# Down projections by seven half-size products whose weight and token sums GpSimd makes

## The reference

```python
x = x + 0.5 * swiglu(rmsnorm(x, g_ffn1), w1_gate, w1_up, w1_down)
x = x + concat(sparse_attention, latent_attention) @ w_out
x = x + 0.5 * swiglu(rmsnorm(x, g_ffn2), w2_gate, w2_up, w2_down)
return rmsnorm(x, g_final)

def swiglu(x, w_gate, w_up, w_down):
    return (jax.nn.silu(x @ w_gate) * (x @ w_up)) @ w_down
```

## Time and profile before

| | us |
|---|---|
| median of 3 runs | 2005.73 |
| lowest and highest | 2002.22, 2006.04 |
| span of the profiled execution | 2001.6 |
| first down projection, as TensorE runs it | 1199.04 to 1318.7, then 1.75 of transposes, to 1320.49 |
| second down projection | 1874.19 to 1993.87 |
| TensorE busy in the whole span | 1924.5 |
| GpSimd busy in the whole span | 196.0 |

### The profile page before, as it was taken

The page is one execution under the profiler, slowest core; times in us unless marked ns, Lnnn a source line. Parts: engine busy times, 40 slices in busy tenths (PEclk is TensorE's granted clock), DMA queues, the critical chain, the costliest instruction groups (busy, mean ns, idle before and its releaser), DMA issues.

```text
span 2001.6 us, 24702 instructions
## 1 busy us (share of the span) xinstructions
PE 1924.5 (96%) x8909; PEld 1345.3 (67%) x8910; DVE 944.0 (47%) x1468; ACT 548.6 (27%) x840; POOL 196.0 (10%) x236
## 2 busy tenths in 40 slices
PE   8999999999997899997999999999999999999998
PEld 7888887884332233333788888886656688888886
DVE  4998983434111111113544443345796444444423
ACT  4234435341000000000522222233337642222222
POOL 2000000001111112111000000001237300000000
PEclk9999999999999999999999999999999999999999
DMA  6444232288999999999333322234110033333332
GB/s 206 151 138 126 85 100 90 84 365 315 425 425 426 427 426 395 421 426 373 94 96 101 97 94 95 93 98 108 60 54 5 12 95 95 94 94 107 102 96 74
DMA packets 153190, 358.70 MB, mean 179 GB/s; under 512 B 31756, under 2 KB 89537, under 8 KB 127898
## 3 DMA queue, kind: packets, MB, share of 16 engines
q1 hardware_dynamic: 147418, 349.64, 47.7%
q0 software_dynamic: 5680, 8.03, 1.1%
q10 hardware_dynamic: 16, 0.00, 0.0%
HBM read 348.29 MB, written 19.40 MB: 184 GB/s over the span
## 4 chain that ended last, share of the span: by engine, by line
PE 78%; SPq 8%; DVE 5%; DMA 4%; ACT 3%; issue 2%; POOL 1%; ACTq 0%; DVEq 0%
PE psum L508 15%; PE psum L510 15%; PE psum L509 15%; PE psum L1356 7%; SPq L1222 6%; PE psum L649 5%; PE psum L651 5%; PE psum L650 5%; PE psum L1366 3%; DMA expert_down_third<-in_w_expert_down_dram 2%; DMA arena<-in_w_expert_down_dram 2%; PE psum L2143 1%; PE psum L2176 1%; DVE arena L2498 1%; SPq L1225 1%
## 5 line engine op out<-in xcount | busy, mean ns | idle before, releaser
L503 DVE TENSOR_TENSOR w_lo<-w_raw,w_hi 128x1024 fp32r<-128x1024 f32 (+1 forms) x232 | 286.9, 1236 | 567.1 <-ACT w_hi L498 567.0
L508 PE MATMUL psum<-h_hi,w_hi 128*128 128x512 f32 x1240 | 488.1, 394 | 3.9 <-DVE h_lo L990 1.9
L510 PE MATMUL psum<-h_hi,w_lo 128*128 128x512 f32 x1240 | 483.4, 390 | 0.0
L509 PE MATMUL psum<-h_lo,w_hi 128*128 128x512 f32 x1240 | 483.1, 390 | 0.0
L498 ACT ACTIVATE w_hi<-w_raw 128x1024 fp32r<-128x1024 f32 (+1 forms) x232 | 245.1, 1056 | 862.1 <-PE psum L510 644.3
L508 PEld LDWEIGHTS psum<-h_hi,w_hi 128*128 128x128 f32 x1240 | 233.2, 188 | 56.7 <-issue 5.2
L509 PEld LDWEIGHTS psum<-h_lo,w_hi 128*128 128x128 f32 x1240 | 233.4, 188 | 49.4 <-issue 1.7
L510 PEld LDWEIGHTS psum<-h_hi,w_lo 128*128 128x128 f32 x1240 | 233.1, 188 | 48.8
L1356 PE MATMUL psum<-arena,w_raw 128*64 128x512 f32 x800 | 181.7, 596 | 13.4 <-DMA arena<-in_w_expert_up_dram 12.5
L1018 DVE SCALAR_TENSOR_TENSOR arena<-arena,vec 128x512 f32<-128x512 f32 x240 | 162.7, 752 | 1.0 <-ACT arena L845 1.0
L1491 ACT ACTIVATE w_raw<-psum 128x256 f32<-128x256 f32 x36 | 13.8, 383 | 461.7 <-PE psum L1356 461.7
(11 more groups left out here) (341 smaller groups left out, 2050.9 us busy)
## 6 DMA issues: line engine op xcount, KB each, us to landing
arena<-in_w_expert_gate_dram SPq DMA_DIRECT2D x44, 1024.0 KB, 23.3
arena<-in_w_expert_up_dram SPq DMA_DIRECT2D x44, 1024.0 KB, 26.2
arena<-in_w_expert_down_dram SPq DMA_DIRECT2D x22, 2048.0 KB, 28.9
w_raw<-in_w_in_dram SPq DMA_DIRECT2D x44, 512.0 KB, 3.7
w_raw<-in_w_gate_dram SPq DMA_DIRECT2D x88, 256.0 KB, 2.8
w_raw<-in_w_up_dram SPq DMA_DIRECT2D x88, 256.0 KB, 3.0
w_raw<-in_w_down_dram SPq DMA_DIRECT2D x44, 512.0 KB, 3.6
expert_down_third<-in_w_expert_down_dram SPq DMA_DIRECT2D x10, 2048.0 KB, 28.0
```

Of the source, the lines that this page charges most:

```text
L503: eng.tensor_tensor(wlo[:, s, :, 0:n], raw[:, slot, :, 0:n], whi[:, s, :, 0:n].bitcast(F32), ALU.subtract).then_inc(w_lo, 1)
L508: eng.matmul(o, w_h, x_h, start=first, stop=False)
L509: eng.matmul(o, w_h, x_l, start=False, stop=False)
L510: return eng.matmul(o, w_l, x_h, start=False, stop=last)
```

## The change

```diff
+            for n in range(4):
+                load_direct(n)
+            for q in range(6):
+                load_terms(q)
+            load_direct(4)
+            load_terms(6)
+            load_terms(7)
+            load_direct(5)
...
+            token_sums(N_UP - 1)
...
+            pool.wait_ge(w_used, C_DN[j])
+            for kp in range(N_UP):
+                difference(kp, kp)
+            for m in range(N_CH):
+                pool.wait_ge(terms_r, N_TERMS * j + min(CK * m + CK, N_UP))
+                pool.wait_ge(w_lo, C_DN[j] + N_CH + m + 1)
+                n, term = pair_size(m), landed(Q_2 + m)
+                pool.tensor_tensor(summed(CK * m, n), summed(CK * m, n), term[:, 0:n, :], ALU.add).then_inc(terms_r, 1)
+            for m in range(N_CH):
+                pool.wait_ge(dx_lo, N_DN * j + m + 1)
+                ks = slice(CK * m, CK * m + pair_size(m))
+                pool.tensor_tensor(act[:, ks, 0, 0:HALF_T], s2[:, ks, :], act[:, ks, 0, 0:HALF_T], ALU.add).then_inc(sums_r, 1)
+            for m in range(N_CH):
+                pool.wait_ge(terms_r, N_TERMS * j + Q_2 + m + 1)
+                pool.wait_ge(w_lo, C_DN[j] + 3 * N_CH + m + 1)
+                n, term = pair_size(m), landed(Q_4 + m)
+                pool.tensor_tensor(summed(CK * m, n), term[:, 0:n, :], summed(CK * m, n), ALU.subtract).then_inc(terms_r, 1)
+            for kp in range(N_UP):
+                pool.wait_ge(w_lo, C_DN[j] + 4 * N_CH + kp // CK + 1)
+                difference(Q_1 + kp, kp)
...
+                for a, t in order:
+                    f, o = slice(t * P, t * P + P), psum[:, banks[prod] + t, :]
+                    begin, end = m == 0 and a == 0, m == N_CH - 1 and a == n - 1
+                    pe.matmul(o, x_h[:, a, f], w_h[:, a, :], start=begin, stop=False)
+                    pe.matmul(o, x_l[:, a, f], w_h[:, a, :], start=False, stop=False)
+                    mm = pe.matmul(o, x_h[:, a, f], w_l[:, a, :], start=False, stop=end)
...
+                act.wait_ge(w_used, C_DN[j] + (x - 1 if x < SPLIT else x - 2 if x >= DSLOTS else 0))
+                act.activation(w_h, weight_of(j, x), ACT.Copy).then_inc(w_hi, 1)
...
+                act.activation(x_h, operand_of(x), ACT.Copy).then_inc(dx_hi, 1)
...
+            for x in range(N_DN):
+                w_h, w_l, x_h, x_l = down_slots(x)
+                if x == 2:
+                    scaled(N_UP - 1)
+                dve.wait_ge(w_hi, C_DN[j] + x + 1)
+                dve.tensor_tensor(w_l, weight_of(j, x), w_h.bitcast(F32), ALU.subtract).then_inc(w_lo, 1)
+                dve.wait_ge(dx_hi, N_DN * j + x + 1)
+                dve.tensor_tensor(x_l, operand_of(x), x_h.bitcast(F32), ALU.subtract).then_inc(dx_lo, 1)
+                after(x)
```

More of the change, by code:

```diff
@@ L1806, in sp_ffn, with load_direct @@
             load_group(N_UP - 1)
+            parts = A[f"w{j + 1}_down_2"].rearrange("o (k e p) n -> p e (o k) n", e=2, p=P)
+            def load_direct(n):
+                m, x = n % N_CH, direct_at(n)
+                e, half = ((0, 0), (1, 0), (1, 1))[n // N_CH]
+                slot = (raw_of(C_DN[j]) + n) % RAW
+                sp.wait_ge(w_lo, C_DN[j] + (direct_at(n - RAW) if n >= RAW else n - RAW) + 1)
+                sp.dma_start(raw[:, slot, 0:pair_size(m), :],
+                             parts[:, e, CK * m:CK * m + pair_size(m), half * CN:half * CN + CN]).then_inc(w_raw[slot], 16)
@@ new lines, in sp_ffn @@
+            for n in range(4):
[6 more added lines that the diff above has]
+            load_direct(5)
+            for q in range(8, Q_2):
+                load_terms(q)
+            for n in range(6, 10):
+                load_direct(n)
+            for q in range(Q_2, Q_4 + 2):
+                load_terms(q)
+            load_direct(10)
+            load_terms(Q_4 + 2)
@@ new lines, in last_rows @@
+            def last_rows():
+                for t in range(2):
+                    if t == 0:
+                        dve.wait_ge(row_done, 2 * (TT - 1) * (j + 1) + j + 1)
+                    else:
+                        dve.wait_ge(w_used, C_DN[j] + N_DN)
+                    rows = rows_tok[:, t, HALF:D]
+                    dve.scalar_tensor_tensor(out=rows, in0=psum[:, 2 + t, :], scalar=0.5, in1=rows, op0=ALU.mult,
+                                             op1=ALU.add).then_inc(evac[(G_DN[j] + 1) % 2] if t else x1_r, 1)
@@ L2674, in act_last @@
             act.activation(stat(V_OFF), stat(R_SUM), ACT.Sqrt)
[L2675 removed]
+            for n, t in enumerate(LAST_ROWS):
                 square_half(act, 3, 1, (t,))
```

439 lines of the change are left out of this document (291 added, 148 removed).

## The result

The changed kernel takes 2067.0 us (median of 4, 2062.9 to 2072.3), the kernel before 2005.5 us in the runs beside it. The ratio is 1.032 (95% interval 1.030 to 1.034): slower by 61.5 us, where 52.7 were forecast. The profiled execution spans 2063.8 us against 2001.6.

A forecast was written before the change was run, and what follows sets the result against it. TensorE bounds the kernel before; in the changed down projections, VectorE and GpSimd excluding each other decides. Products sum to 146 us against 119.7, +26.4 per stage, +52.7 for two on 2005.7: 2058 us, range 2022 to 2090.

The forecast's parts named there:

- turns: Down projections: VectorE instructions with two SBUF inputs and GpSimd's exclude each other, 3.85 to 4.0 us per chunk against 2.72.
- the stall: Product 0 of each down projection: TensorE idles 8 to 10 us before chunk 4, whose load queues behind term loads.

## What to carry over

Before moving elementwise work to GpSimd beside a VectorE that reads two SBUF operands, price each meeting at GpSimd's whole instruction, twice a step if two such VectorE instructions lie in it; VectorE doing the work itself can be the cheaper place (2052.9 for 2067.0 us, with two of four sums moved), and one operand in PSUM frees it. In a load queue, a load that waits for nothing goes ahead of every load that waits for the engine you are adding work to; but moving it gives back only what nothing else holds up (6 of 12 us a stage here). A fast algorithm that saves 12% of the matmuls has to leave each chunk's preparation under the shortened matmul time, turns included.

## What the runs showed of the hardware

TensorE's granted clock around the stall (windows of 5 us, columns as above):

```profile
1916.00:1921.00 5.00, 2.99 (x12) 2.17 (x12) 1.10 (x1) 0.00 (x0) 4.84 (x6) 1.00 0.56 207
1921.00:1926.00 5.00, 0.00 (x0) 0.00 (x0) 0.00 (x0) 0.00 (x0) 3.68 (x3) 0.95 0.79 264
1926.00:1931.00 5.00, 0.00 (x0) 0.00 (x0) 1.85 (x2) 1.58 (x2) 2.87 (x2) 0.50 1.05 407
1931.00:1936.00 5.00, 3.81 (x10) 3.03 (x11) 5.00 (x4) 2.40 (x4) 5.00 (x4) 0.53 0.92 318
1936.00:1941.00 5.00, 3.97 (x18) 2.98 (x17) 5.00 (x5) 3.96 (x5) 2.52 (x2) 1.00 1.04 401
```

After nearly 12 us without a matmul TensorE comes back at 1.2 GHz (0.50): the first eight matmuls of chunk 4 are some 0.43 us apart instead of 0.227, and the chunk takes 4.47 us instead of 2.72. It is back at 2.4 GHz by the last window. That costs 1.75 us of TensorE's time and none of the stage's: after chunks 4 and 5 it waits for VectorE again, 1.03 us before chunk 6:

```profile
1939.21 0.47 PE L2033 MATMUL psum<-w_hi,down_operands 128*128 128x512 f32 x1 [1.03 <-DVE down_operands L2248]
```
